# The first weight sum of a seven-product duo made by an accumulating transfer instead of an addition by POOL

## The chip, the cores and the metric

The kernel runs on one core of a Trainium2 chip. Its time is the device time of one execution in microseconds (us); the kernel before takes 1981.56 us, the median of 3 runs between 1980.24 and 1981.6. The five engines of the core are TensorE (PE in the profile; PEld is its loading of weights), VectorE (DVE), ScalarE (ACT), GpSimd (POOL) and SyncE (SP), which here only issues DMA transfers. Each has its own instruction stream and waits for the others through semaphores.

## The reference

The kernel is one layer of a hybrid encoder on 592 tokens (64 of a sample stream, 528 of a prompt) of width 1024. The layer begins and ends with a half step of a gated feed-forward network (FFN), and the change touches these two alone:

```python
def swiglu(x, w_in, w_out):
    a, b = jnp.split(x @ w_in, 2, axis=-1)
    return (jax.nn.silu(a) * b) @ w_out

def layer(h, lw, ...):
    h = h + 0.5 * swiglu(rmsnorm(h, lw['norm_ffn1']), lw['ffn1_w_in'], lw['ffn1_w_out'])
    ...   # combined input projection, a state-space branch, an attention branch, a gated merge
    h = h + 0.5 * swiglu(rmsnorm(h, lw['norm_ffn2']), lw['ffn2_w_in'], lw['ffn2_w_out'])
```

`w_in` is 1024 x 5632 (2816 gate columns, then 2816 columns of the other factor), `w_out` is 2816 x 1024, all in float32.

## The kernel before

**Duos.** The weights stream through SBUF in duos. A duo of `w_in` is 128 gate columns and the 128 columns 2816 further on, over all 8 row tiles of 128: two loads of 512 KB into one of the two slots of `raw` (`pair`, called by SP's `ffn`). A duo of `w_out` is 256 columns. An FFN runs in four parts (`PARTS`): 6, 6, 6 and 4 duos of `w_in`, each part followed by its 4 duos of `w_out`. FFN1 works on 592 columns of tokens, FFN2 on 576 (the 16 meta tokens are gone).

**High and low halves.** Each float32 factor is split into a float32r upper half, made by ACT (`wh`), and the rest, made by DVE (`wl` = weight - `wh`). PE multiplies three of the four combinations.

**Seven products.** Apart from the first duos (`PLAIN_IN`: 2 in FFN1, 1 in FFN2), a duo of `w_in` is fast: its weights are cut into 2 x 2 blocks (row tiles odd or even, gate columns or the others), the tokens into 2 x 2 blocks too, and 7 block products stand in place of 8, each of 12 matmuls. There are 20 fast duos in FFN1 (4, 6, 6, 4 by part) and 21 in FFN2 (5, 6, 6, 4). `chunk(slot, n, k)` is a block: n is 1 for the gate columns and 2 for the others, k is 1 for the odd and 2 for the even row tiles. Four weight sums are needed:

- the first, `sums[:, 0]` = `chunk(2,1)` + `chunk(2,2)`, by POOL (L908), 
- the second, `sums[:, 1]` = the first - `chunk(1,1)`, by DVE (`sum_2`, L1643), 
- the third, written over `chunk(2,1)`, by POOL (L911), after the second, 
- the fourth, `sums[:, 2]` = `chunk(1,2)` - the second, by DVE (`sum_4`, L1648).

There is one `sums` tile for each FFN, so the first sum of a duo may be written only when the duo before it no longer needs its own: when DVE has made that one's low halves from `sums`.

**The low and high halves of a fast duo** are made in three pieces: x (the gate columns as they are, products 0 and 1), y (`sums`, products 2 to 4) and z (the other columns, products 5 and 6). ACT makes the upper pieces (`upper_x` L1160, `upper_y` L1166, `upper_z` L1172), DVE the lower (`lower_x` L1654, `lower_y` L1659, `lower_z` L1665). PE waits for `lower_y` ahead of product 2 (`wl_part`), and for `lower_z` ahead of product 5. The places in `wh` and `wl` are single too: ACT may write the upper y piece of the next duo only when PE has finished product 4, the fifth, of this one.

**What DVE does while PE works on a fast duo**, in this order: `gate_b` of the duo before (L1687, L1690), `lower_z` of this one, `sum_2` of the next, `hidden_lower` of the one before (L1698), `lower_x` and `sum_4` of the next, `gate_a` of this one (L1676, L1677, from products of PE), `lower_y` of the next. Each engine does its instructions in the written order.

**Loads.** SP issues the pair of the duo after next as soon as `lower_z` of this one has freed its slot (`split_done`), and waits for nothing else in between. POOL, in its own `ffn`, takes the first sum as soon as the duo is loaded (`raw_ready`) and `sums` is free, then waits for `sum_2` and makes the third.

Of the kernel before, what the change touches and what calls it, by code (L numbers as in the profile page):

```python
# [8 lines left out]
ALU = mybir.AluOpType  # L9
# [4 lines left out]
P = 128  # L14
# [8 lines left out]
FF = 2816  # L23
# [35 lines left out]
PLAIN_IN = (2, 1)  # L59
FF_TILES = FF // P  # L60
# [55 lines left out]
def duos_of(ffn):  # L116
    d, i, c, out = (FF_TILES - PLAIN_IN[0]) * ffn, FF_TILES * ffn, 0, []
    for part, (_, nt) in enumerate(PARTS):
        for into, count in ((True, nt), (False, 4)):
            for n in range(count):  # L120
                fast = into and len(out) >= PLAIN_IN[ffn]
                out.append(Duo(ffn, len(out), into, part, n, fast, d, i, c))
                d, i, c = d + fast, i + into, c + (not fast)
    return out


FFN_DUOS = [duos_of(0), duos_of(1)]
# [239 lines left out]
def fox_ssd_hybrid_kernel(nc, x_prompt, x_sample, cache_k, cache_v, cache_logf, state_ssm, state_conv,  # L367
# [6 lines left out]
    with ctx:  # L374
# [3 lines left out]
        def sem(name):  # L378
            return ctx.enter_context(nc.semaphore(name))
# [59 lines left out]
        with ExitStack() as s:  # L439
            half = HALF  # L440
            F1 = {"half": HALF, "tok": TOK}
# [88 lines left out]
        with ExitStack() as s:  # L530
            G2 = {"half": DENSE // 2, "tok": DENSE}
# [22 lines left out]
        def apart(slot):  # L554

            return raw[:, slot, :, :].rearrange("p (k e) c -> p e k c", e=2)

        def chunk(slot, n, k):

            return apart(slot)[:, k - 1, :, (n - 1) * P:n * P]  # L560
# [49 lines left out]
        stage_in = [sem("stage_in0"), sem("stage_in1")]  # L610
        finb_ready = sem("finb_ready")
        wh_part, wl_part, prod_done, snap_ready = sem("wh_part"), sem("wl_part"), sem("prod_done"), sem("snap_ready")
        s1_made, s2_made, s3_made, s4_made = sem("s1_made"), sem("s2_made"), sem("s3_made"), sem("s4_made")
        c_done, hid_made, hid_hi, hid_ready = sem("c_done"), sem("hid_made"), sem("hid_hi"), sem("hid_ready")
        gk_ready, xt_first, xt_made = sem("gk_ready"), sem("xt_first"), sem("xt_made")
# [32 lines left out]
        def raw_loads(duo, slots):  # L648
            slot = slots[duo.s]
            return 32 * (USES[duo.ffn][slot] + duo.q // 2 + 1)  # L650
# [41 lines left out]
        def _(sp):  # L692
# [3 lines left out]
            def load(slot, parts):  # L696

                sp.wait_ge(split_done, st.duo(PRIMED - 1))
                for dst, src in parts:
                    sp.dma_start(dst, src).then_inc(raw_ready[slot], 16)  # L700
                st.duo.up()
                st.uses[slot].up()

            def r(slot, k0, k1, c0, c1):
                return raw[:, slot, k0:k1, c0:c1]
# [5 lines left out]
            def pair(s, w, c, apart):  # L711
                load(s, [(r(s, 0, KT, 0, P), w[:, :, bass.ds(c, P)]),
                         (r(s, 0, KT, P, 256), w[:, :, bass.ds(c + apart, P)])])

            def ffn(e, win, wout, slots):
                for duo in FFN_DUOS[e]:
                    t0, nt = PARTS[duo.part]
                    s = slots[duo.q % 2]
                    if duo.into:
                        if e == 0 and duo.q == 1:  # L720
                            sp.wait_ge(x_in[1], 16 * 5)
                        pair(s, win, (t0 + duo.n) * P, FF)
                    else:
                        c, m = duo.n * 256, nt // 2
                        load(s, [(r(s, 0, m, 0, 256), wout[:, t0:t0 + m, bass.ds(c, 256)]),
                                 (r(s, m, nt, 0, 256), wout[:, t0 + m:t0 + nt, bass.ds(c, 256)])])
# [137 lines left out]
            for f in range(2, KT + 1, 2):  # L864
                c = slice((f - 2) * P, f * P)
# [11 lines left out]
        def _(pool):  # L877
# [18 lines left out]
                pool.tensor_tensor(G["xtlf"][:, k, 0, :], halfway(gk, 2, half), halfway(gk, 1, half), ALU.subtract).then_inc(xt_first, 1)  # L896

            def ffn(e, G, slots):
                duos = FFN_DUOS[e]
                pool.wait_ge(ss_ready, (1, 3)[e])  # L900
                for duo in duos:
                    if not duo.fast:
                        continue
                    slot = slots[duo.s]
                    before = duos[duo.q - 2] if duo.q > 1 else None
                    pool.wait_ge(raw_ready[slot], raw_loads(duo, slots))
                    pool.wait_ge(wl_part, 2 * duo.d)
                    pool.tensor_tensor(G["sums"][:, 0, :].rearrange("p (k c) -> p k c", k=4), chunk(slot, 2, 1), chunk(slot, 2, 2), ALU.add)\  # L908
                        .then_inc(s1_made, 1)
                    pool.wait_ge(s2_made, duo.d + 1)  # L910
                    pool.tensor_tensor(chunk(slot, 2, 1), chunk(slot, 1, 1), chunk(slot, 2, 1), ALU.subtract).then_inc(s3_made, 1)  # L911

# [136 lines left out]
            n = X_MIX + KT  # L1049
# [507 lines left out]
        def _(dve):  # L1557
# [77 lines left out]
            def ffn(e, slots):  # L1635
                last = e == 1
                half, duos = G["half"], FFN_DUOS[e]
                actb, full, hh, hl, sums = G["act"], G["full"], G["hh"], G["hl"], G["sums"]
                rs = in_halves(G["rs"][:, :])

                def sum_2(duo):
                    dve.wait_ge(s1_made, duo.d + 1)
                    dve.tensor_tensor(sums[:, 1, :].rearrange("p (k c) -> p k c", k=4), sums[:, 0, :].rearrange("p (k c) -> p k c", k=4),  # L1643
                                      chunk(slots[duo.s], 1, 1), ALU.subtract).then_inc(s2_made, 1)

                def sum_4(duo):
                    dve.wait_ge(s2_made, duo.d + 1)
                    dve.tensor_tensor(sums[:, 2, :].rearrange("p (k c) -> p k c", k=4), chunk(slots[duo.s], 1, 2),  # L1648
                                      sums[:, 1, :].rearrange("p (k c) -> p k c", k=4), ALU.subtract).then_inc(s4_made, 1)

                def lower_x(duo):

                    dve.wait_ge(wh_part, 2 * duo.d + 1)
                    dve.tensor_tensor(two_places(wl, 0), column(slots[duo.s], 1), two_places(wh, 0).bitcast(F32), ALU.subtract).then_inc(wl_part, 1)  # L1654
# [62 lines left out]
                for duo in duos:  # L1717
                    q, prev = duo.q, duos[duo.q - 1] if duo.q else None
                    after = duos[q + 1] if q + 1 < len(duos) else None
                    if duo.fast:  # L1720
                        if prev.into:
                            gate_b(prev)
                        lower_z(duo)
                        if after.fast:
                            sum_2(after)
                        if prev.into:
                            hidden_lower(prev)
                        if after.fast:
                            lower_x(after)
                            sum_4(after)  # L1730
                        else:
                            lower_plain(after)
                        gate_a(duo)
                        if after.fast:
                            lower_y(after)
                    elif duo.into:
                        if q == 0:
                            inverse()
                        else:
                            gate_b(prev)  # L1740
                        if after.fast:
                            sum_2(after)
                            sum_4(after)
                        gate_a(duo)
                        if q:
                            hidden_lower(prev)
                            if after.fast:
                                lower_x(after)
                        if after.fast:
                            lower_y(after)  # L1750
                    else:
                        if duo.n == 0:
                            gate_b(prev)
                            hidden_lower(prev)
                        if after is None:
                            if not last:
                                split(0, cols=48)
                        elif after.fast:
                            sum_2(after)
                            sum_4(after)  # L1760
                            lower_x(after)
                            lower_y(after)
                        else:
                            lower_plain(after)
                        for u in range(2):
                            m = 2 * duo.n + u
                            add_out(duo, u)
                            if duo.part == len(PARTS) - 1 and m:
                                if not last:
                                    lower_g(xul, xuh, m - 1, NORM_MIX)  # L1770
                                gather(m - 1, full)
# [10 lines left out]
            G = F1  # L1782
# [215 lines left out]
            G = G2  # L1998
# [505 lines left out]
```

## Time and profile before

| | |
|---|---|
| time, median of 3 runs | 1981.56 us |
| the profiled execution | 1983.64 us, its span on the core 1982.0 us |
| granted TensorE clock, mean | 0.991 of full speed |
| PE, DVE, ACT, POOL busy | 97%, 61%, 48%, 28% of the span |
| HBM read | 168.89 MB |

A span runs from the first to the last instruction of the program; the rest of the time of an execution lies around it. Times in the rows below are microseconds from the span's start. FFN1 lies at about 34 to 445 us, FFN2 at about 1528 us to the end. A wait is read from the idle time that stands in brackets behind an instruction, with the instruction that ended it.

### The profile page before, as it was taken

The page shows a single profiled execution, that of the slowest core. Times are in us where ns is not written, and L with a number is a line of the kernel's source. Part 1 is how long each engine was busy: PE and PEld are TensorE (multiplying, and loading weights), DVE is VectorE, ACT ScalarE, POOL GpSimd, SP SyncE. Part 2 cuts the span into 40 slices and gives each one's busy share as a digit, 9 for nine tenths or more (in the row PEclk, how much of TensorE's full clock was granted, in tenths as well). Part 3 has the DMA queues.
Part 4 walks back from the last instruction along what each step waited for, and adds up shares of the span by engine and source line. Part 5 has one row for each costly group of instructions (what it writes and reads, how often), then busy time and mean ns, then how long its engine had stood idle before and what let it go on. Part 6 is the DMA issues. An engine that isn't in the chain of part 4 may idle for free. (4 is left out here: it accounts for less than half of the span.)

```text
span 1982.0 us, 35663 instructions
## 1 busy us (share of the span) xinstructions
PE 1919.9 (97%) x14315; PEld 1868.8 (94%) x14315; DVE 1206.0 (61%) x1869; ACT 947.3 (48%) x1807; POOL 559.3 (28%) x606
## 2 busy tenths in 40 slices
PE   5999999997999999999999999999999999999997
PEld 5999999997999989998999999999999999999996
DVE  5868686777663466346634662223444796968685
ACT  6525353445565566546654665333222462525244
POOL 2202021205744264426442643223111121202010
PEclk9999999998999999999999999999999999999998
DMA  5233323223325222522252225224333233323322
GB/s 138 59 91 86 107 65 107 75 79 102 97 79 179 68 70 75 180 67 74 70 180 67 81 64 173 85 65 155 124 103 124 65 93 90 90 91 86 106 70 64
DMA packets 226946, 190.51 MB, mean 96 GB/s; under 512 B 11136, under 2 KB 215232, under 8 KB 225632
## 3 DMA queue, kind: packets, MB, share of 16 engines
q1 hardware_dynamic: 221824, 173.76, 28.9%
q0 software_dynamic: 4416, 14.32, 2.4%
q8 instruction: 113, 1.85, 0.4%
q14 instruction: 49, 0.40, 0.1%
q10 hardware_dynamic: 544, 0.17, 0.0%
HBM read 168.89 MB, written 19.33 MB: 95 GB/s over the span
## 5 line engine op out<-in xcount | busy, mean ns | idle before, releaser
L2081 PE MATMUL ps<-xah,wh 128*128 128x296 f32 (+1 forms) x1696 | 377.7, 304 | 9.9 <-DVE xal L1586 5.8
L2081 PE MATMUL ps<-xah,wl 128*128 128x296 f32 (+1 forms) x1696 | 376.8, 304 | 0.0
L2081 PE MATMUL ps<-xal,wh 128*128 128x296 f32 (+1 forms) x1696 | 371.4, 301 | 0.0
L978 POOL TENSOR_TENSOR wl<-raw,wh 128x512 fp32r<-128x512 f32 (+1 forms) x184 | 232.9, 1273 | 407.8 <-ACT wh L1101 407.5
L2081 PEld LDWEIGHTS ps<-xah,wh 128*128 128x128 f32 x1696 | 274.7, 190 | 12.2 <-DVE xal L1586 5.0
L2081 PEld LDWEIGHTS ps<-xal,wh 128*128 128x128 f32 x1696 | 276.1, 190 | 0.0
L2081 PEld LDWEIGHTS ps<-xah,wl 128*128 128x128 f32 x1696 | 274.7, 190 | 0.1
L2145 PE MATMUL ps<-xth,wh 128*128 128x296 f32 (+1 forms) x656 | 194.8, 297 | 1.7 <-DVE wl L1659 1.7
L2145 PE MATMUL ps<-xth,wl 128*128 128x296 f32 (+1 forms) x656 | 194.8, 297 | 0.0
L2145 PE MATMUL ps<-xtl,wh 128*128 128x296 f32 (+1 forms) x656 | 194.5, 296 | 0.0
L908 POOL TENSOR_TENSOR sums<-raw 128x512 f32<-128x512 f32 x41 | 53.0, 1294 | 415.6 <-DMA raw<-in_ffn_w_in_dram 214.6
L2093 PE MATMUL ps<-wh,xal 128*128 128x256 f32 (+1 forms) x440 | 128.0, 291 | 0.0
L2093 PE MATMUL ps<-wh,xah 128*128 128x256 f32 (+1 forms) x440 | 125.6, 286 | 1.2 <-ACT zr L1356 1.2
L2145 PEld LDWEIGHTS ps<-xth,wh 128*128 128x128 f32 x656 | 123.7, 189 | 1.9 <-DVE wl L1659 1.9
L2093 PE MATMUL ps<-wl,xah 128*128 128x256 f32 (+1 forms) x440 | 124.9, 284 | 0.0
L2145 PEld LDWEIGHTS ps<-xtl,wh 128*128 128x128 f32 x656 | 123.7, 189 | 0.0
L2145 PEld LDWEIGHTS ps<-xth,wl 128*128 128x128 f32 x656 | 123.6, 188 | 0.0
L911 POOL TENSOR_TENSOR raw<-raw 128x512 f32<-128x512 f32 x41 | 69.4, 1693 | 175.2 <-DVE sums L1643 175.2
L1321 ACT ACTIVATE pt<-ps 128x640 f32<-128x640 f32 (+4 forms) x80 | 42.9, 537 | 151.7 <-PE ps L2175 151.7
L1101 ACT ACTIVATE wh<-raw 128x512 fp32r<-128x512 f32 (+1 forms) x192 | 110.4, 592 | 0.2
L1905 DVE SCALAR_TENSOR_TENSOR cvt<-xp,parh,cvt 128x595 f32<-128x595 f32 x96 | 98.7, 1029 | 18.9 <-ACT cvt L1421 17.0
L1817 DVE RECIPROCAL rinv<-rsum 128x1 f32<-128x1 f32 (+1 forms) x80 | 13.0, 163 | 149.2 <-PE ps L2238 149.2
(334 smaller groups left out, 4708.2 us busy)
## 6 DMA issues: line engine op xcount, KB each, us to landing
raw<-in_ffn_w_in_dram SPq DMA_DIRECT2D x88, 512.0 KB, 5.0
raw<-in_w_in_dram SPq DMA_DIRECT2D x80, 512.0 KB, 4.5
raw<-in_ffn_w_out_dram SPq DMA_DIRECT2D x48, 384.0 KB, 3.6
brow<-acs_rows SPq DMA_DIRECT2D x8, 1184.0 KB, 6.1
raw<-in_w_br_ssm_dram SPq DMA_DIRECT2D x16, 512.0 KB, 4.4
bias<-bias_rows SPq DMA_DIRECT2D x32, 160.0 KB, 5.4
os_spill<-yT SPq DMA_DIRECT2D x8, 592.0 KB, 3.0
bias<-biasp_rows SPq DMA_DIRECT2D x16, 264.0 KB, 5.5
```

The source lines that it names most:

```text
L908: pool.tensor_tensor(G["sums"][:, 0, :].rearrange("p (k c) -> p k c", k=4), chunk(slot, 2, 1), chunk(slot, 2, 2), ALU.add)\
L911: pool.tensor_tensor(chunk(slot, 2, 1), chunk(slot, 1, 1), chunk(slot, 2, 1), ALU.subtract).then_inc(s3_made, 1)
L978: ins = pool.tensor_tensor(wl[:, slot, k, 0:cols], raw[:, slot, k, 0:cols], wh[:, slot, k, 0:cols].bitcast(F32), ALU.subtract)
L1101: act.activation(wh[:, slot, k, 0:cols], raw[:, slot, k, 0:cols], ACT.Copy).then_inc(hi_ready if c == 3 else hi_part, 1)
L1321: act.activation(pt[:, k % 2, :].rearrange("p (b q) -> p b q", b=TILES)[:, 0:nb, 0:m], bank(6, TILES * P).rearrange("p (b q) -> p b q", b= ...
L1817: link(dve.reciprocal(rinv[0:m, k % 4:k % 4 + 1], rsum[0:m, k % 4:k % 4 + 1]))
L1905: ins = dve.scalar_tensor_tensor(out=c, in0=xp[:, j, tap:tap + CO], scalar=parh[:, bass.ds(conv_tile(i, g, j) + 32 * tap, 1)], in1=c, op0= ...
L2081: ins = pe.matmul(bank(b + a, half), as_row(w)[:, at + 256 * k + j * P:at + 256 * k + (j + 1) * P], x[:, k, a * half:(a + 1) * half], star ...
L2093: ins = pe.matmul(bank(b, 256, m), x[:, k, t * P:t * P + m], w[:, slot, k, :], start=(k == 0 and w is wh and x is xh), stop=(k == KT - 1 a ...
L2145: ins = pe.matmul(bank(duo.b + b, half), as_row(w)[:, 512 * p + P * k:512 * p + P * (k + 1)], operand(name, k, low), start=(start and k == ...
```

## The change

For all fast duos but the first of each FFN (39 of 41), SP loads the block `chunk(2,1)` a second time, from HBM into `sums[:, 0]`: one transfer of 128 partitions x 4 row tiles x 128 columns, 256 KB. It is issued behind the pair of the same duo and waits until `sums` is free (`wl_part`, on SP now). When it has landed (`odd_in`), POOL issues a transfer from SBUF to SBUF that adds `chunk(2,2)` onto it (`accum_op=ALU.add`). When that has landed (`s1_in`), DVE's `sum_2` may go on. On DVE, `sum_2` of the next duo moves behind `hidden_lower` and `lower_x` where the current duo is fast.

```diff
--- before.py
+++ after.py
@@ -610,6 +610,7 @@
         stage_in = [sem("stage_in0"), sem("stage_in1")]
         finb_ready = sem("finb_ready")
         wh_part, wl_part, prod_done, snap_ready = sem("wh_part"), sem("wl_part"), sem("prod_done"), sem("snap_ready")
+        odd_in, s1_in = sem("odd_in"), sem("s1_in")
         s1_made, s2_made, s3_made, s4_made = sem("s1_made"), sem("s2_made"), sem("s3_made"), sem("s4_made")
         c_done, hid_made, hid_hi, hid_ready = sem("c_done"), sem("hid_made"), sem("hid_hi"), sem("hid_ready")
         gk_ready, xt_first, xt_made = sem("gk_ready"), sem("xt_first"), sem("xt_made")
@@ -720,6 +721,11 @@
                         if e == 0 and duo.q == 1:
                             sp.wait_ge(x_in[1], 16 * 5)
                         pair(s, win, (t0 + duo.n) * P, FF)
+                        if duo.fast and duo.q > PLAIN_IN[e]:
+                            c = (t0 + duo.n) * P + FF
+                            sp.wait_ge(wl_part, 2 * duo.d)
+                            sp.dma_start((F1, G2)[e]["sums"][:, 0, :].rearrange("p (k c) -> p k c", k=4),
+                                         win.rearrange("p (k a) n -> p k a n", a=2)[:, :, 0, c:c + P]).then_inc(odd_in, 16)
                     else:
                         c, m = duo.n * 256, nt // 2
                         load(s, [(r(s, 0, m, 0, 256), wout[:, t0:t0 + m, bass.ds(c, 256)]),
@@ -896,7 +902,7 @@
                 pool.tensor_tensor(G["xtlf"][:, k, 0, :], halfway(gk, 2, half), halfway(gk, 1, half), ALU.subtract).then_inc(xt_first, 1)
 
             def ffn(e, G, slots):
-                duos = FFN_DUOS[e]
+                duos, loaded = FFN_DUOS[e], e * (FF_TILES - PLAIN_IN[0] - 1)
                 pool.wait_ge(ss_ready, (1, 3)[e])
                 for duo in duos:
                     if not duo.fast:
@@ -904,9 +910,14 @@
                     slot = slots[duo.s]
                     before = duos[duo.q - 2] if duo.q > 1 else None
                     pool.wait_ge(raw_ready[slot], raw_loads(duo, slots))
-                    pool.wait_ge(wl_part, 2 * duo.d)
-                    pool.tensor_tensor(G["sums"][:, 0, :].rearrange("p (k c) -> p k c", k=4), chunk(slot, 2, 1), chunk(slot, 2, 2), ALU.add)\
-                        .then_inc(s1_made, 1)
+                    s1, even = (G["sums"][:, 0, :].rearrange("p (k c) -> p k c", k=4), chunk(slot, 2, 2))
+                    if duo.q > PLAIN_IN[e]:
+                        loaded += 1
+                        pool.wait_ge(odd_in, 16 * loaded)
+                        pool.dma_start(s1, even, accum_op=ALU.add).then_inc(s1_in, 16)
+                    else:
+                        pool.wait_ge(wl_part, 2 * duo.d)
+                        pool.tensor_tensor(s1, chunk(slot, 2, 1), even, ALU.add).then_inc(s1_made, 1)
                     pool.wait_ge(s2_made, duo.d + 1)
                     pool.tensor_tensor(chunk(slot, 2, 1), chunk(slot, 1, 1), chunk(slot, 2, 1), ALU.subtract).then_inc(s3_made, 1)
 
@@ -1639,7 +1650,10 @@
                 rs = in_halves(G["rs"][:, :])
 
                 def sum_2(duo):
-                    dve.wait_ge(s1_made, duo.d + 1)
+                    if duo.q > PLAIN_IN[last]:
+                        dve.wait_ge(s1_in, 16 * (duo.d - last))
+                    else:
+                        dve.wait_ge(s1_made, last + 1)
                     dve.tensor_tensor(sums[:, 1, :].rearrange("p (k c) -> p k c", k=4), sums[:, 0, :].rearrange("p (k c) -> p k c", k=4),
                                       chunk(slots[duo.s], 1, 1), ALU.subtract).then_inc(s2_made, 1)
 
@@ -1721,12 +1735,11 @@
                         if prev.into:
                             gate_b(prev)
                         lower_z(duo)
-                        if after.fast:
-                            sum_2(after)
                         if prev.into:
                             hidden_lower(prev)
                         if after.fast:
                             lower_x(after)
+                            sum_2(after)
                             sum_4(after)
                         else:
                             lower_plain(after)
```

POOL's stream at the start of FFN1's fast duos: `sums<-raw` is the first sum, `raw<-raw` the third. Before:

```order
L908 TENSOR_TENSOR sums<-raw 128x512 [waits wl_part,raw_ready0,ss_ready]
L911 TENSOR_TENSOR raw<-raw 128x4x128 [waits s2_made]
L908 TENSOR_TENSOR sums<-raw 128x512 [waits wl_part,raw_ready1]
L911 TENSOR_TENSOR raw<-raw 128x4x128 [waits s2_made]
L908 TENSOR_TENSOR sums<-raw 128x512 [waits wl_part,raw_ready0]
```

The same place in the changed kernel:

```order
L920 TENSOR_TENSOR sums<-raw 128x512 [waits wl_part,raw_ready0,ss_ready]
L922 TENSOR_TENSOR raw<-raw 128x4x128 [waits s2_made]
L917 DMA sums<-raw 128x4x128 [waits odd_in,raw_ready1]
L922 TENSOR_TENSOR raw<-raw 128x4x128 [waits s2_made]
L917 DMA sums<-raw 128x4x128 [waits odd_in,raw_ready0]
```

From the second fast duo on, the addition is a transfer that POOL issues, and it waits for SP's second load instead of for `sums`.

DVE's stream over one fast duo of FFN1, from `lower_y` (the first row) to the next `lower_y` (the last). Before:

```order
L1659 TENSOR_TENSOR wl<-sums,wh 128x1536 [waits wh_part]
L1687 TENSOR_TENSOR full<-ps,full 128x592 [waits prod_done,snap_ready]
L1690 TENSOR_TENSOR full<-full,act 128x592 [waits gated,c_done]
L1665 TENSOR_TENSOR wl<-raw,wh 128x1024 [waits hi_ready]
L1643 TENSOR_TENSOR sums<-sums,raw 128x512 [waits s1_made]
L1698 TENSOR_TENSOR hl<-full,hh 128x592 [waits hid_hi]
L1654 TENSOR_TENSOR wl<-raw,wh 128x1024 [waits wh_part]
L1648 TENSOR_TENSOR sums<-raw,sums 128x512 [waits s2_made]
L1676 TENSOR_TENSOR act<-ps,act 128x592 [waits prod_done,snap_ready]
L1677 TENSOR_TENSOR act<-act,rs 128x592 [waits dch]
L1659 TENSOR_TENSOR wl<-sums,wh 128x1536 [waits wh_part]
```

The same stretch in the changed kernel:

```order
L1673 TENSOR_TENSOR wl<-sums,wh 128x1536 [waits wh_part]
L1701 TENSOR_TENSOR full<-ps,full 128x592 [waits prod_done,snap_ready]
L1704 TENSOR_TENSOR full<-full,act 128x592 [waits gated,c_done]
L1679 TENSOR_TENSOR wl<-raw,wh 128x1024 [waits hi_ready]
L1712 TENSOR_TENSOR hl<-full,hh 128x592 [waits hid_hi]
L1668 TENSOR_TENSOR wl<-raw,wh 128x1024 [waits wh_part]
L1657 TENSOR_TENSOR sums<-sums,raw 128x512 [waits s1_in]
L1662 TENSOR_TENSOR sums<-raw,sums 128x512 [waits s2_made]
L1690 TENSOR_TENSOR act<-ps,act 128x592 [waits prod_done,snap_ready]
L1691 TENSOR_TENSOR act<-act,rs 128x592 [waits dch]
L1673 TENSOR_TENSOR wl<-sums,wh 128x1536 [waits wh_part]
```

`sum_2` (L1643, now L1657) stands two instructions later, straight ahead of `sum_4`, and waits for the accumulating transfer.

## Rows read from the trace of the kernel before

**Rows 1.** The page, busy time of each engine over the span.
```profile
PE 1919.9 (97%) x14315; PEld 1868.8 (94%) x14315; DVE 1206.0 (61%) x1869; ACT 947.3 (48%) x1807; POOL 559.3 (28%) x606
```

**Rows 2.** Waits of PE over the whole run: line, released by, us, times, longest.
```profile
...
PE ps L2145 <- DVE wl L1659: 1.7, 1, 1.7
...
```

**Rows 3.** Timeline of DVE, one duo: start, us, instruction, idle before.
```profile
...
164.94 0.68 DVE L1643 TENSOR_TENSOR sums<-sums,raw 128x512 f32<-128x512 f32 x1
...
168.46 0.68 DVE L1648 TENSOR_TENSOR sums<-raw,sums 128x512 f32<-128x512 f32 x1
170.00 0.78 DVE L1676 TENSOR_TENSOR act<-ps,act 128x592 f32<-128x592 f32 x1 [0.86 <-PE ps L2145]
170.81 0.78 DVE L1677 TENSOR_TENSOR act<-act,rs 128x592 f32<-128x592 f32 x1
171.51 1.76 DVE L1659 TENSOR_TENSOR wl<-sums,wh 128x1536 fp32r<-128x1536 f32 x1
...
```

**Rows 4.** Timeline of ACT, the same duo, the upper y piece.
```profile
...
169.99 1.49 ACT L1166 ACTIVATE wh<-sums 128x1536 fp32r<-128x1536 f32 x1 [1.30 <-PE ps L2145]
...
```

**Rows 5.** Timeline of POOL, the same duo.
```profile
161.96 1.29 POOL L908 TENSOR_TENSOR sums<-raw 128x512 f32<-128x512 f32 x1 [6.99 <-DVE wl L1659]
165.70 1.75 POOL L911 TENSOR_TENSOR raw<-raw 128x512 f32<-128x512 f32 x1 [2.45 <-DVE sums L1643]
```

**Rows 6.** Timeline of SP, the same duo: the pair's two loads.
```profile
165.04 0.99 SPq L700 DMA_DIRECT2D raw<-in_ffn_w_in_dram  x2
```

**Rows 7.** Timeline of PE: first matmul of product 2, six fast duos.
```profile
164.79 0.30 PE L2145 MATMUL ps<-xth,wh 128*128 128x296 f32 x1
...
176.24 0.30 PE L2145 MATMUL ps<-xth,wh 128*128 128x296 f32 x1
...
1587.62 0.40 PE L2145 MATMUL ps<-xth,wh 128*128 128x288 f32 x1 [1.65 <-DVE wl L1659]
...
1598.97 0.29 PE L2145 MATMUL ps<-xth,wh 128*128 128x288 f32 x1
...
1693.10 0.29 PE L2145 MATMUL ps<-xth,wh 128*128 128x288 f32 x1
...
1704.24 0.29 PE L2145 MATMUL ps<-xth,wh 128*128 128x288 f32 x1
```

**Rows 8.** Timeline of DVE: two further lower y pieces.
```profile
145.51 1.75 DVE L1659 TENSOR_TENSOR wl<-sums,wh 128x1536 fp32r<-128x1536 f32 x1
...
1699.65 1.76 DVE L1659 TENSOR_TENSOR wl<-sums,wh 128x1536 fp32r<-128x1536 f32 x1
```

**Rows 9.** DMA issues, whole run: engine, count, KB each, median us to landing.
```profile
...
raw<-in_ffn_w_out_dram SPq DMA_DIRECT2D x16, 256.0 KB, 2.9
raw<-in_w_in_dram SPq DMA_DIRECT2D x16, 256.0 KB, 3.2
...
h<-h_spill POOLq DMA_DIRECT2D x8, 256.0 KB, 2.9
...
h<-oa_spill POOLq DMA_DIRECT2D x1, 768.0 KB, 8.7
...
h<-h_spill POOLq DMA_DIRECT2D x8, 32.0 KB, 2.0
...
raw<-in_w_in_dram SPq DMA_DIRECT2D x1, 128.0 KB, 2.4
...
```

**Rows 10.** DMA issues, 1383 to 1385 us: POOL's transfers behind a pair.
```profile
...
full<-os_spill POOLq DMA_DIRECT2D x1, 256.0 KB, 4.0
full<-os_spill POOLq DMA_DIRECT2D x1, 32.0 KB, 4.0
```

**Rows 11.** POOL's issues by line: ns min/median/max; one row a partition, then several.
```profile
L1067 POOL DMA_DIRECT2D h<-h_spill x16: 535/537/539, 1477.7 to 1522.6; - x16
...
L1035 POOL DMA_DIRECT2D h<-oa_spill x4: 768/856/899, 1271.3 to 1349.4; - x4
```

**Rows 12.** SP's loads by line L700, 145 to 200 us: landing times.
```profile
...
DMA to landing us min/median/max: 3.7/4.2/5.2
```

## The prediction

> **What bounds the kernel now.** I read the page first, for the busiest engine: PE works 97% of the span, POOL 28% [rows 1]. Then the waits of PE over the whole run, for the lines of the seven products: behind `lower_y` PE waits once, for 1.7 us [rows 2], at the first fast duo of FFN2, which keeps POOL's addition. So in the stages that the change touches PE runs without a break, and what POOL does there costs no time. The reader should therefore not ask what POOL's 1.29 us are worth, but how late the first sum may come before PE notices.
>
> That is read from the timelines of one duo, in the order in which its work is handed on. Product 2 begins at 164.79 and, one duo later, at 176.24 [rows 7]: a duo takes PE 11.45 us in FFN1, and 1704.24 - 1693.10 = 11.14 us in FFN2. The `lower_y` that the second of these needs ends at 171.51 + 1.76 = 173.27 [rows 3], 2.97 us early; in FFN2 it ends at 1699.65 + 1.76 = 1701.41 [rows 8], 2.83 us early. What sets it is PE itself: ACT's upper y piece starts at 169.99 after an idle time that PE ended [rows 4], while `sum_4` had been done at 168.46 + 0.68 = 169.14 [rows 3]. The first sum is far from setting anything: it starts at 161.96, 0.15 us after the `lower_y` before it ended [rows 5], and lasts 1.29.
>
> **The change part by part.** The profiled execution took 1983.64 us for a span of 1982.0; it lies 2.1 us above the median of the runs, and the sum is carried over to that median.
>
> *Removed:* 39 of POOL's 41 additions, 39 x 1.29 = 50 us of POOL's time [rows 5]. PE's work covers all of it: 0 us.
>
> *Moved:* `sum_2` behind `lower_x`. By itself this costs nothing, since `sum_4` does not move, and it ended 0.85 us ahead of ACT's start. POOL's third sum (1.75 us [rows 5]) now starts later too; it is wanted only at the next duo's products 5 and 6, and stays covered.
>
> *Added on SP:* 39 loads of 256 KB, each waiting for `lower_y` of the duo before. Queued behind each is the next pair; but that pair waits for `lower_z`, which DVE does after that `lower_y`, so it is not held. The price of such a load is between 2.4 us (half its size) and 3.2 us (its size and form, but two issued together) [rows 9]; I take 2.9, a load of its size.
>
> *Added on POOL:* 39 accumulating transfers. Behind each waits the third sum, which needs `sum_2`, and so this transfer, anyway. The trace shows no accumulating transfer. From below: a plain POOL transfer of 256 KB with nothing beside it lands after 2.9 us [rows 9]. From above: an addition moves each byte three times (two reads, one write), and 768 KB by POOL took 8.7 us [rows 9]. The nearest row is the one with a pair of SP's in flight, because here too the pair is issued at 165.04 [rows 6], 3.2 us after `lower_y` ended, just when the second load has landed and POOL issues: 256 KB took 4.0 us there [rows 10]. To it I add the second operand, 1.0 us (224 KB more cost 2.9 - 2.0 = 0.9 [rows 9]), and 0.3 us for an issue of several rows a partition (0.86 against 0.54 us [rows 11]). That makes A = 5.3 us, an estimate.
>
> On the price of the transfer the Trainium skill has a rule of its own ("DMA: Bandwidth & Descriptors", "Anatomy of one DMA — SWDGE (gpsimd) path"): a POOL transfer takes about 2.0 us plus its bytes at 436 GB/s. The rows with nothing beside them agree (32 KB in 2.0, 256 KB in 2.9); for an addition beside a pair that would be an estimate of about 3.2 us, and the sum below would be nothing.
>
> *The loop.* Before, the chain from one `lower_y` to the next had room because its first step took 1.3 us. Now there is one `sums` tile and two transfers in a row in the chain: `lower_y` ends, the second load (2.9), the accumulating transfer (A), `sum_2` 0.68, `sum_4` 0.68, `gate_a` 0.78 + 0.78 = 1.56 (ACT's upper y piece, 1.49, lies beside it), `lower_y` 1.76 [rows 3], and three hand-overs at 0.15 each, 0.45. That is 2.9 + A + 5.13, and with A = 5.3 it is 13.33 us, against PE's 11.45 and 11.14. Each duo, `lower_y` comes 1.88 us (FFN1) or 2.19 us (FFN2) later against PE. In a part this begins with the third fast duo: the first two are prepared while PE works on `w_out` (`lower_y` of one first duo ends at 147.26 [rows 8], 17.5 us before PE wants that of the second at 164.79 [rows 7]). Until PE waits, the 2.97 or 2.83 us are used up. So:
> - a part of six duos has 4 links: 4 x 1.88 - 2.97 = 4.55 us in FFN1, twice, 9.1; 4 x 2.19 - 2.83 = 5.93 in FFN2, twice, 11.9;
> - a part of four has 2 links: 0.79 in FFN1, twice (its first part is counted so too), 1.6; 1.55 in FFN2;
> - FFN2's first part has no room at its start: `lower_y` of its first fast duo is what PE waits for at 1587.62, and wants the next at 1598.97 [rows 7], 11.35 us later. 4 links: 13.33 - 11.35 = 1.98, and 3 x 2.19 = 6.57: 8.5 us.
>
> The sum is 32.6 us: 2016.2 us for the profiled execution, 2014 us for the median.
>
> **The rivals.**
>
> *The two transfers fit.* If the accumulating transfer lands in at most 3.8 us, the loop is at most 11.83 us; in parts of six the room eats the links, FFN2's first part loses 0 to 2.6 us, and all the rest under 0.5. Time 1981.6 to 1985, about 1983: not slower by more than 0.2% (4 us, about what a measurement of this kernel can tell). It decides at A = 3.9, where the sum reaches 4 us. For it speaks the plain row of 2.9 us; against it the 4.0 us of the same size behind a pair, before a byte of the second operand is counted. By the skill's rule above this is what happens.
>
> *POOL's transfer waits for the whole pair.* In the stretch of rows 10 both of POOL's transfers, 32 KB and 256 KB, landed after 4.0 us, where they take 2.0 and 2.9 alone: the small one waited for something. If that is SP's queue emptying first, then here the accumulating transfer moves only when the pair has landed, 3.2 + 0.5 + 5.2 = 8.9 us after `lower_y` (the issue, the second load's issue behind the first, the longest landing [rows 6, 12]), and takes 1.9 us more for two times 256 KB, with A = 10.8 - 3.2 = 7.6. The loop is then 15.63 us, 4.18 and 4.49 us over PE's: FFN1 2 x 5.39 + 2 x 13.75 = 38.3, FFN2 (4.28 + 13.47) + 2 x 15.13 + 6.15 = 54.2, together 92 us: 2074 us. With the upper bound A = 8.7 it would be 121 us and 2103. Against it speaks that the 256 KB of rows 10 were late by only 1.1 us.
>
> Of two queues the Trainium skill says (the same page, "Queues, rings and completion order") that a DMA engine goes round the queues that have work, packet by packet. By that the small transfer should not have doubled its time; the row leans the other way. It would put the time near my forecast and not at this rival's.
>
> *POOL's addition slows others.* If its 1.29 us on shared paths to SBUF held up PE, the change would give that back. PE waits nowhere in these parts but the 1.7 us of rows 2, which stay; a gain above 0.2% would have to come out of PE's own pace, for which no row speaks. At most 2 us: 1979.5.
>
> **How the numbers follow.** The forecast, a loop between 12 and 14.5 us (A from 3.9 to 6.5, a time of 1986 to 2045), has 0.50; the fitting transfers 0.20; the transfer behind the pair, with all above 2045, 0.25; a gain through POOL 0.03; the remaining 0.02 goes to a change that does something else than it says, without a sign. The prediction is 2014 us. The range takes in the fitting transfers and goes up to A = 7.1 (loop 15.13: FFN1 2 x 4.39 + 2 x 11.75 = 32.3, FFN2 15.75 + 2 x 13.13 + 5.15 = 47.2, 2061 us): 1980 to 2062. Faster by over 0.2%: 0.03; within it: 0.19; slower: 0.78.
>
> **What would show it right or wrong.** The landing of the second load (2.4 to 3.2 us) and of the accumulating transfer (5.3) stand among the DMA issues. DVE's idle time before `sum_2` should be ended by that transfer, and PE's waits at the line of the seven products, behind `lower_y`, should rise from 1.7 us to about 30, in the later duos of each part, growing from none at the second; from one `lower_y` to the next in such a part there should be 13.3 us. If `sum_2` does not wait, or PE does not, the loop fits, and I have set the transfer too high. If the accumulating transfer's first packets come only after the pair's last, the second rival holds. And if PE waits elsewhere (for `lower_z`, or a pair that came late), my chain was not the one that decides.

## The result, and the profile after

The changed kernel takes 2046.14 us (median of 4 runs, 2045.63 to 2050.07) against 1981.58 beside it: 1.0332 times as long, with a 95% interval of 1.0319 to 1.0344, 64.6 us more. The forecast was 2014 us in a range of 1980 to 2062: the sign and the mechanism hold, but the rise forecast, 32 us, was only half of the one that came. The profiled span grew from 1982.0 to 2044.0 us, by 62.0.

First the busy times of the page, to set beside [rows 1].

```profile
PE 1938.2 (95%) x14315; PEld 1878.6 (92%) x14315; DVE 1168.6 (57%) x1869; ACT 936.7 (46%) x1807; POOL 563.0 (28%) x606
```

PE has the same 14315 matmuls and a smaller share. POOL is not relieved: each of its 39 DMA instructions counts 1.29 us, as much as the addition that it replaces [rows 5]. DVE's busy time even fell by 37 us, most of it at `lower_x`: in the duo of [rows 3] that took 2.31 us (at 166.23), beside POOL's third sum of [rows 5], and in the duo below, without it, it takes 1.22. That gains nothing, because DVE had idle time before, at 61% busy. The work is the same; PE waits, and after some waits runs at a lower clock (below). Its waits in the whole run, at the line of the seven products (L2145 before), answer to [rows 2]:

```profile
PE ps L2158 <- DVE wl L1673: 47.2, 28, 3.6
...
PE ps L2158 <- DVE wl L1668: 3.2, 1, 3.2
```

From 1.7 us in one wait to 47.2 in 28, behind `lower_y`. (The second line, behind `lower_x`, is not new: 3.2 us stood there before as well.) Who held `lower_y`? DVE in FFN2's first part, from the `lower_y` of the third fast duo to that of the fourth (start, us, instruction, idle time before it and what ended it):

```profile
1638.68 1.75 DVE L1673 TENSOR_TENSOR wl<-sums,wh 128x1536 fp32r<-128x1536 f32 x1
...
1643.61 1.22 DVE L1668 TENSOR_TENSOR wl<-raw,wh 128x1024 fp32r<-128x1024 f32 x1
1649.92 0.69 DVE L1657 TENSOR_TENSOR sums<-sums,raw 128x512 f32<-128x512 f32 x1 [5.09 <-DMA sums<-raw]
1650.64 0.69 DVE L1662 TENSOR_TENSOR sums<-raw,sums 128x512 f32<-128x512 f32 x1
1651.26 0.75 DVE L1690 TENSOR_TENSOR act<-ps,act 128x576 f32<-128x576 f32 x1
1652.04 1.07 DVE L1691 TENSOR_TENSOR act<-act,rs 128x576 f32<-128x576 f32 x1
1653.03 1.75 DVE L1673 TENSOR_TENSOR wl<-sums,wh 128x1536 fp32r<-128x1536 f32 x1
```

Before, `gate_a` waited for PE [rows 3]; now `sum_2` waits 5.09 us for the transfer, and from there to the second `lower_y` DVE goes on without a break. The steps in between are SP's loads and POOL's issue in the same duo:

```profile
1640.45 0.37 SPq L727 DMA_DIRECT2D sums<-in_ffn_w_in_dram  x1
1643.05 0.99 SPq L701 DMA_DIRECT2D raw<-in_ffn_w_in_dram  x2
```

```profile
1643.78 1.30 POOL L917 DMA_DIRECT2D sums<-raw  x1 [5.64 <-DMA sums<-in_ffn_w_in_dram]
```

`lower_y` ends at 1640.43 and SP issues the second load 0.02 us later. It lands at 1643.12. POOL starts its instruction 0.66 us after that, and 0.73 us behind the pair that SP issued at 1643.05. The transfer lands 6.12 us later, at 1649.90, and the next `lower_y` ends at 1654.78: a loop of 14.35 us, in which 9.5 are the two transfers and the hand-over between them. The DMA issues (KB each, median us to landing) show the same over all 39:

```profile
sums<-in_ffn_w_in_dram SPq DMA_DIRECT2D x39, 256.0 KB, 2.8
sums<-raw POOLq DMA_DIRECT2D x39, 256.0 KB, 5.2
```

The 5.2 is a median over several kinds. For the first two duos of each part behind a part of `w_out` (12 transfers), no pair is under way when POOL issues; they land after 4.3 to 5.2 us and lie outside the loop. The loop has the 26 links of the forecast. In 18 of them the transfer follows a pair of `w_in` and lands after 6.2 us in the mean (4.9 to 7.4); in the other 8, for the last duo of a part, it follows the smaller loads of `w_out` and lands after 5.0 (4.3 to 6.1). The mean of all 26 is a loop of 14.34 us (12.7 to 15.6): 2.9 for the second load, 0.6 from its landing to POOL's issue, 5.9 for the transfer, 4.9 from there to the end of `lower_y`.

What the transfer does in its 6.1 us is seen in the packets of each queue (packets, MB, share of the 16 engines). From POOL's issue to 1647.4, only SP's queue has packets:

```profile
q1 hardware_dynamic: 1911, 0.97, 94.9%
issues: line engine op xcount, KB each, median us to landing
raw<-in_ffn_w_in_dram SPq DMA_DIRECT2D x1, 512.0 KB, 5.1
sums<-raw POOLq DMA_DIRECT2D x1, 256.0 KB, 6.1
```

and from 1648.2 to 1649.6, apart from one load of code, only POOL's:

```profile
q0 software_dynamic: 337, 0.16, 94.7%
...
```

POOL's first packet moves 3.65 us after the issue, its last ends after 5.78; the pair's last ends after 4.33. So the two overlap for 0.7 us and no more: for its first 3.65 us the accumulating transfer stands behind a pair issued 0.73 us before it. All 19 transfers that follow a pair of `w_in` show the same: POOL issues them 0.5 to 1.8 us behind the pair, and their first packet comes 4.3 to 4.5 us after the pair's issue, whenever POOL's own was. POOL's instruction takes 1.3 us here as it does with no pair beside it, so it is not the issuing that is slow.

Where the 62 us arose, part by part, from the ends of the `lower_y` of both traces (how much later it stands at the start of the next part than at the start of this one; the last part from the growth of the span), beside the sum of the forecast:

| part | forecast, loop 13.33 | same sum, loop 14.4 | measured |
|---|---|---|---|
| FFN1, four fast duos | 0.8 | 2.9 | 3.8 |
| FFN1, six | 4.6 | 8.8 | 9.7 |
| FFN1, six | 4.6 | 8.8 | 8.8 |
| FFN1, four | 0.8 | 2.9 | 1.1 |
| FFN2, five behind a plain one | 8.5 | 12.8 | 11.7 |
| FFN2, six | 5.9 | 10.2 | 10.5 |
| FFN2, six | 5.9 | 10.2 | 13.5 |
| FFN2, four | 1.6 | 3.7 | 2.1 |
| sum | 32.6 | 60.3 | 61.2 |

(0.8 us stand in front of the first part.) The shape of the forecast is right: in each of the six parts behind a part of `w_out` the second duo comes at the old distance (14.6 and 14.1 us in both traces), the loss begins with the third, and a part with more links loses more. Only the loop is longer.

Not all of this is PE standing still: its busy time grew too, by 18.3 us for the same matmuls [rows 1]. A duo with a wait in it counts about 0.5 us more of busy time even at a granted clock of 1.00 (11.65 us from 1625.94 to 1640.43, where a duo took 11.14 before [rows 7]); why, no run here shows. And in five of the 26 links PE goes on after a wait at half its clock for a while. First the end of one wait on PE, then windows around it (us, busy us and instructions of PE, PEld, DVE, ACT, POOL, granted clock, DMA share, GB/s):

```profile
1640.48 0.40 PE L2158 MATMUL ps<-xth,wh 128*128 128x288 f32 x1 [2.83 <-DVE wl L1673]
```

```profile
1634.00:1640.40 6.40, 3.65 (x28) 3.42 (x26) 4.75 (x6) 3.10 (x4) 1.78 (x1) 1.00 0.17 20
1641.80:1645.10 3.30, 3.30 (x16) 3.30 (x15) 3.03 (x4) 1.93 (x3) 1.30 (x1) 0.50 0.47 139
1645.30:1652.00 6.70, 6.70 (x53) 6.70 (x52) 2.05 (x3) 1.04 (x2) 1.30 (x1) 1.00 0.73 154
```

In the second window PE is busy throughout at a granted clock of 0.50, the 1.2 GHz level, and does 16 matmuls in 3.30 us; in the third it has 2.4 GHz again. That delay comes out of the next wait, not on top of it, as long as PE's duo with it (12.96 us busy in this link) stays under the loop (14.35 us here).

### The profile page after: what moved, and what is told of

Same layout as the page of the kernel before. It is cut to its first block and busy times, and to the rows that moved or that the text cites. A ratio compares the mean times of both kernels' runs of the same rounds, so it can differ in the third digit from the quotient of the medians.

```text
span 2044.0 us, 35702 instructions
## 1 busy us (share of the span) xinstructions
PE 1938.2 (95%) x14315; PEld 1878.6 (92%) x14315; DVE 1168.6 (57%) x1869; ACT 936.7 (46%) x1807; POOL 563.0 (28%) x606
## 3 DMA queue, kind: packets, MB, share of 16 engines
q0 software_dynamic: 25008, 24.55, 6.6%
## 5 line engine op out<-in xcount | busy, mean ns | idle before, releaser
L2158 PE MATMUL ps<-xth,wh 128*128 128x296 f32 (+1 forms) x656 | 201.8, 308 | 47.2 <-DVE wl L1673 47.2
L2158 PE MATMUL ps<-xtl,wh 128*128 128x296 f32 (+1 forms) x656 | 198.8, 303 | 0.0
L917 POOL DMA_DIRECT2D sums<-raw x39 | 50.5, 1294 | 392.3 <-DMA sums<-in_ffn_w_in_dram 386.2
L1177 ACT ACTIVATE wh<-sums 128x1536 fp32r<-128x1536 f32 x41 | 61.1, 1490 | 184.5 <-DVE sums L1662 166.1
```

The lines of the kernel that those rows point to most:

```text
L917: pool.dma_start(s1, even, accum_op=ALU.add).then_inc(s1_in, 16)
L1177: act.activation(places(wh, 2, 3), G["sums"][:, :, :].rearrange("p s c -> p (s c)"), ACT.Copy).then_inc(wh_part, 1)
L2158: ins = pe.matmul(bank(duo.b + b, half), as_row(w)[:, 512 * p + P * k:512 * p + P * (k + 1)], operand(name, k, low), start=(start and k == ...
```

## The experiments

The theory after the result: one loop runs through the single first sum, its time is about 14.4 us, and POOL's transfer is long in it for two reasons, the addition and the pair ahead of it. Rivals: a price for each transfer wherever it lies (contention, SP's queue), the moved `sum_2`, or the second load alone.

**The addition back on POOL, the second load kept** (and `sum_2` waits for POOL's instruction again).

```diff
-                        pool.dma_start(s1, even, accum_op=ALU.add).then_inc(s1_in, 16)
+                        pool.tensor_tensor(s1, s1, even, ALU.add).then_inc(s1_made, 1)
```

> The changed kernel with the second load, but POOL adds the even block onto it by an instruction (1.3 us) and not by a transfer. Theory (the second load alone, 2.8 us, fits into the room): a loop of 2.8 + 0.2 + 1.3 + 4.9 = 9.2 us, under PE's period, no wait of PE in the fast duos but the old ones, 1980 to 1985 us. Rival (the second load's 10 MB or its wait on SP is what costs): 1995 us or more.

Measured: 1981.01 us, ratio 0.9997 (0.9988 to 1.0006). PE's wait behind `lower_y` is the one of before:

```profile
PE ps L2155 <- DVE wl L1670: 1.7, 1, 1.7
```

So 10 MB more on SP's queue, the wait of SP and the later first sum cost nothing. What costs is what the transfer takes beyond 1.3 us.

**A second tile for the first sum**, used by every other duo, so that the second load may start one duo earlier (the y piece of these duos is made by two instructions).

```diff
-                            sp.wait_ge(wl_part, 2 * duo.d)
+                            sp.wait_ge(wl_part, 2 * (duo.d - 1))
...
-                    s1, even = (G["sums"][:, 0, :].rearrange("p (k c) -> p k c", k=4), chunk(slot, 2, 2))
+                    s1, even = (first_sum(G, duo).rearrange("p (k c) -> p k c", k=4), chunk(slot, 2, 2))
```

> The changed kernel with a second tile for the first sum, used by every other fast duo: the second load is issued right behind its pair and waits for the lower y piece of the duo before last, not of the last. The price: for every other duo ACT and DVE make the y piece in two instructions. Theory (the time went into a loop through one sums tile: lower y piece, second load, accumulating transfer, sum_2, sum_4, lower y piece, 14.4 us against PE's 11.45 or 11.15): the loop is cut, both transfers run ahead, PE waits behind the lower y piece as before the change (about 2 us in all), 1980 to 1988 us. Rival (the added traffic itself slows the loads or PE, whatever the order): PE still waits, 2010 us or more.

Measured: 1981.18 us, ratio 0.9999 (0.999 to 1.0008). The waits and the DMA issues:

```profile
PE ps L2169 <- DVE wl L1684: 1.7, 1, 1.7
```

```profile
odd<-raw POOLq DMA_DIRECT2D x20, 256.0 KB, 4.2
...
sums<-raw POOLq DMA_DIRECT2D x19, 256.0 KB, 4.2
```

All 39 accumulating transfers are there, with every byte that they move, and the loss is gone: it belongs to the loop and not to the transfers. The second loads take 5.5 us here, because now it is they that lie beside the pair; nobody waits for them. With it the accumulating transfers, at 4.2 us, hardly lie beside a pair any more: this run takes that wait away too. What it is worth by itself is measured further down, and it is not the whole loss.

**Every other transfer**, 20 of the 39; the other sums by POOL as before.

```diff
-                    if duo.q > PLAIN_IN[e]:
-                        loaded += 1
-                        pool.wait_ge(odd_in, 16 * loaded)
+                    if by_transfer(duo):
+                        pool.wait_ge(odd_in, 16 * so_far(duo))
```

Here `by_transfer` is true of the fast duos with an odd number in their part (but for the first of FFN2), and SP's load and DVE's wait follow the same test.

> The changed kernel, but only every other fast duo of a part (the 2nd, 4th and 6th, 20 of 41) takes the transfer; the others take POOL's addition as before the change. Theory (a loop of 14.4 us that first eats 2.97 or 2.84 us of room; a duo by POOL's addition gets 0.6 to 0.9 us of it back): a part of six loses 1 us in FFN1 and 3 us in FFN2, the first parts 2.6 and 3.5 us, the last parts nothing: about 14 us, 1996 us (1990 to 2002). Rival (each transfer costs a fixed share, 64.6 / 39 = 1.66 us): 33 us, 2015 us.

Measured: 1992.06 us, ratio 1.0055 (1.004 to 1.007); PE's waits:

```profile
PE ps L2165 <- DVE wl L1680: 5.9, 7, 1.7
...
PE ps L2165 <- ACT full L1212: 3.2, 6, 0.6
```

The second line, six short waits for ACT, stands in no other run; what causes it is not shown. Loops of 9.8 and of 13.2 to 15.4 us take turns. A fixed price per transfer, 64.6 / 39 = 1.66 us, would have given 33 us for 20; it is about 11. Half the transfers cost a sixth, because a short loop between two long ones gives most of the room back.

**The pair kept away from the transfer**: SP issues the next pair only when the accumulating transfer has landed.

```diff
+                            sp.wait_ge(s1_in, 16 * (duo.d - e))
```

> The changed kernel, but SP issues the next pair only when the accumulating transfer has landed. Theory (POOL's transfer lands late, 6.2 us after its issue, because its queue gets nothing while a pair of 1 MB is on the move): it lands after about 4.4 us, the loop is 12.6 us instead of 14.4, and the time is about 1999 us (1990 to 2010). Rival (the addition in the transfer is slow by itself): it lands after about 6 us all the same, the loop stays over 14 us, and the time is 2040 us or more.

**The transfer as a plain copy**, the pair left where it was.

```diff
-                        pool.dma_start(s1, even, accum_op=ALU.add).then_inc(s1_in, 16)
+                        pool.dma_start(s1, even).then_inc(s1_in, 16)
```

> The changed kernel with a plain copy in place of the accumulating transfer; the addition of the odd block is left out. Theory (the wait behind the pair is most of the landing time, and the addition adds about 1 us to moving the bytes): it lands after about 5.3 us, the loop is 13.5 us, about 2027 us (2018 to 2036). Rival (the addition is what is slow): about 4 us, a loop of 12.2 us, 1990 to 2000 us. If the addition costs nothing: 6.2 us and 2046 us.

**Both edits together.**

> Both edits together: the next pair waits for POOL's transfer, and that is a plain copy (the addition of the odd block is left out). Theory: with nothing beside it the copy lands after 2.7 us, the loop is 2.9 + 0.55 + 2.7 + 4.85 = 11.0 us, at or under PE's period, 1981 to 1986 us; so the addition's own price is 4.2 - 2.7 = 1.5 us, and neither it nor the wait behind the pair alone makes the whole loss. Rival (the pairs that come later are what costs in the kernel where they wait): 2000 us or more here as well.

All three times lie in the ranges expected, the first at its edge. With the changed kernel these make a square. A is the time from POOL's issue to the landing; A and the loop are means over the 26 links:

| | beside the pair | pair held back |
|---|---|---|
| accumulating | A 5.9, loop 14.3, 2046.1 us | A 4.4, loop 13.0, 2009.6 us (1.0145, 1.0129 to 1.016) |
| plain copy | A 5.4, loop 14.0, 2034.7 us (1.0267, 1.0247 to 1.0286) | A 2.8, loop 11.5, 1982.4 us (1.001, 1.0001 to 1.0019) |

PE's waits and POOL's transfers with the pair held back and the addition kept:

```profile
PE ps L2159 <- DVE wl L1674: 20.7, 17, 2.4
```

```profile
sums<-raw POOLq DMA_DIRECT2D x39, 256.0 KB, 4.2
```

as a plain copy beside the pair:

```profile
PE ps L2158 <- DVE wl L1673: 36.2, 20, 3.6
```

and as a plain copy with the pair held back:

```profile
PE ps L2159 <- DVE wl L1674: 2.0, 2, 1.7
```

```profile
sums<-raw POOLq DMA_DIRECT2D x39, 256.0 KB, 2.7
```

Either cause alone is enough for a loss; only without both does the loop fit, to within 0.2% of the time. Of the two the pair weighs more: holding it back takes 36.5 us off, leaving out the addition 11.4. Beside the pair even the plain copy, which moves for 1.5 us, takes most of the accumulating one's time. The accumulating kernel with the pair held back was expected at 1999 us and took some 10 us more: some of its loops last 13.8 to 14.5 us in place of 12.5 to 13, and some of its transfers 5.3 to 5.9 us with no pair beside them. Its trace shows what was beside them: loads of the kernel's own code (queue q8, 16 KB each). The 28 accumulating transfers with none in flight land after 4.16 to 4.23 us; of the 11 with one, nine take 4.45 to 5.89. In the loop the second load, too, is late (3.3 to 4.3 us) only with one in flight. Over the 26 links the means are 0.20 us above 4.20 for the transfer and 0.12 above 2.95 for the second load, some 8 us in all by an estimate from these. No run here takes the code loads away.

**The moved `sum_2` alone**, on the kernel before.

```diff
-                        if after.fast:
-                            sum_2(after)
                         if prev.into:
                             hidden_lower(prev)
                         if after.fast:
                             lower_x(after)
+                            sum_2(after)
                             sum_4(after)
```

> The kernel before with the one edit that sum_2 stands behind hidden_lower and lower_x; POOL adds as before. Theory: sum_4 and the upper y piece keep their times, no difference beyond 0.2% (1979 to 1984 us). Rival: sum_2's later start makes the third sum and so the z piece late, slower by 4 us or more.

Measured: 1981.08 us, ratio 1.0 (0.9991 to 1.0009). The move costs nothing, as forecast.

**And taken back in the changed kernel**, with `sum_2` again ahead of `hidden_lower` and `lower_x`:

> The changed kernel with sum_2 back in its old place on DVE, ahead of hidden_lower and lower_x. Theory: what DVE does between sum_2 and sum_4 (0.8 us and 1.2 to 2.3 us) then stands behind the wait for the transfer and joins the loop, 17 us instead of 14.4: about 2115 us (2095 to 2130). Rival (the place of sum_2 does not matter, the transfer alone sets the time): 2046 us.

Measured: 2125.93 us, ratio 1.0728 (1.0712 to 1.0745), 80 us more than the changed kernel. PE now waits for something else:

```profile
PE ps L2159 <- DVE wl L1668: 100.6, 28, 5.2
...
PE ps L2159 <- DVE wl L1673: 3.4, 6, 1.6
```

With `sum_2` in front, `hidden_lower` and `lower_x` queue on DVE behind a wait for the transfer, and the loop lasts 17.1 us. The move is what keeps the changed kernel's loss down.

No version beats the kernel before: where the loop is cut PE works through these parts as it did, and POOL's time was not on the path.

## Why the prediction was right and wrong

*Right:* the removed additions bring nothing; the move is free; the second load costs nothing by itself; the loop through the one `sums` tile decides, from the third duo of a part on, with PE waiting behind `lower_y`. The second load was put at 2.9 us and took 2.9 in the mean of the 26 links (2.8 in the median); `sum_2`, `sum_4`, `gate_a` and `lower_y` with their hand-overs ran in 4.9 us, about as read from [rows 3].

*The step that failed* is the price of the transfer, "the nearest row is the one with a pair of SP's in flight", from which A = 5.3 us came; behind a pair of `w_in` it was 6.2, over all 26 links 5.9. I took the 4.0 us of [rows 10] for a price, to which the second operand is added. They are a landing that hangs on the pair's. There POOL issued the 32 KB at 1383.96, 1.21 us behind SP's pair, whose two loads landed after 3.5 and 4.4 us, and the 256 KB 0.58 us later still; its first packet came 4.15 us after the pair's issue, much as here (4.3 to 4.5). Here POOL issues 0.73 us behind a pair whose second load takes 5.1. The two do not start together, as the prediction has it: POOL starts later, by the hand-over below, and the pair comes 2.62 us after `lower_y` in place of 3.2 [rows 6], because the second instruction of `gate_b` takes 0.76 us (at 1641.13) without POOL's addition beside it, where it took 1.26 (at 162.62). A plain copy of the size of [rows 10] takes 5.8 us in this place (mean of 18 links), not 4.0. That is close to the second rival's mechanism, "POOL's transfer waits for the whole pair", though not by the sign that I had named for it: the first packets come 0.7 us before the pair's last in the duo shown, not after it. I had given it 0.25 and held against it that the 256 KB "were late by only 1.1 us"; the 32 KB ahead of it, late by 2.0 us, were the row to trust. Its price of 7.6 us was too high: in the duo shown the pair had landed 4.8 us after POOL's issue, for which the rival has 5.7, and the transfer landed 1.4 us behind it, not 1.9. So the time came out between the two cases, at 2046, just past the border of 2045 that I had drawn between them.

On this point the Trainium skill says ("DMA: Bandwidth & Descriptors", "Queues, rings and completion order") that a DMA engine goes round the queues that have work for it, packet by packet. The trace does not show that between these two: in 3.6 us q1 moved 1911 packets and q0, whose transfer was issued at the start of that stretch, none. Of these 3.6 us some 1.9 are the transfer's own start, as the accumulating transfer without a pair shows; the rest is waiting, and what withholds q0's turn the trace does not show. For the landing of a POOL transfer the Trainium skill has 2.0 us plus the bytes at 436 GB/s (the same page, "Anatomy of one DMA — SWDGE (gpsimd) path"): an estimate by it is 2.6 us for 256 KB, which the plain copy alone meets with 2.7; the accumulating one takes 4.2 alone, where an estimate with twice the bytes would make 3.2.

*A second term* was too small: a hand-over of 0.15 us each. From `lower_y` to SP's issue and from the transfer's landing to `sum_2` it is even less, 0.02 us in the duo shown; from the landing of a load to POOL's DMA instruction waiting on it, it is 0.55 us in the median and 0.6 in the mean. The two make the loop 14.34 us in the mean in place of 13.33: about 0.55 more for A, 0.45 for the hand-over. That A counts for no more, though it was 0.9 us off behind a pair of `w_in`, is owed to the 8 links behind the smaller loads of `w_out`, which the prediction had not set apart.

*Why 8% of a loop doubled the sum:* only what exceeds PE's period counts, over 26 links, and the room of each part had already been taken off. 26 x 1.01 = 26 us on top of 32.6 is 59 us of the 62.0 by which the span grew. The remaining 3 us are within what the parts of the table differ by from the sum.

## What to carry to other kernels

An engine at 28% is not a reason to move its work to a transfer: ask for the loop that the work stands in, add up its steps with the transfer's landing time, and compare with the period of the engine that bounds. A buffer that is written by a transfer and freed at the end of a chain closes such a loop; a second buffer opens it again, and that cost nothing here. A landing time read beside another queue's transfer is no price to carry over: see when its first packet moved, and what had been issued just before it.

## What the runs showed of the hardware

- A transfer of POOL issued 0.73 us after 1 MB on SP's queue moved nothing for 3.65 us; alone its first packet came after 1.9. Behind a pair of `w_in` the first packet came 4.3 to 4.5 us after the pair's issue, in 19 of 19 cases. Being small does not help: [rows 10], 32 KB in 4.0 us.
- An accumulating transfer is cut finer than a plain one. Of q0's packets in the whole run (4416 before, 25008 after, 7536 with plain copies) each of the 39 accumulating transfers has 528 and each plain copy 80, for the same 256 KB. With nothing beside it it moves in 2.0 us against 1.0, and POOL's instruction takes 1.29 us against 0.76.
- A DMA instruction of POOL starts 0.55 us after the landing that it waited for (median of 39), 0.66 in the duo shown.
- With the pair held back, an accumulating transfer landed after 4.16 to 4.23 us (28 of 28) with no load of the kernel's code in flight, and after 4.45 to 5.89 in nine of 11 with one of 16 KB.
- DVE's `lower_x` took 2.31 us beside POOL's third sum and 1.22 without it.
- After a wait of 2.83 us PE ran for about 3.4 us at a granted clock of 0.50; after two others, of 2.65 and 2.82 us, it did not. The mean granted clock went from 0.991 to 0.988 only.
